# Forget gates' projection: high and low halves of eight weight columns in one stationary operand

## What is computed

```python
h = rmsnorm(x, norm_g[l])
proj = h @ w_in[l]
(cv_a, cv_b, cv_gate, fq, fk, fv, f_logit, fox_gate,
 mq, mem_gate) = jnp.split(proj, SPLITS, axis=-1)
...
logf = jax.nn.log_sigmoid(f_logit.astype(jnp.float32) + b_f[l].astype(jnp.float32))
y_fox = fox_attention(fq.reshape(shp), fk.reshape(shp), fv.reshape(shp), logf)
...
mkv = rmsnorm(mem, mem_norm_g[l]) @ w_mem_kv[l]
```

## Time and profile before

| | |
|---|---|
| median of 3 runs | 1925.85 us (1925.09 to 1926.88) |
| the profiled execution | 1928.19 us |
| its span, first to last instruction | 1926.4 us |
| busy: TensorE, VectorE, ScalarE, GpSimd | 98%, 58%, 40%, 10% |
| mean granted TensorE clock | 0.996 of full speed |
| the three products of a projection, 512 columns | 2288 of each, 931.8 + 893.9 + 894.4 us busy |
| chain that ended last | TensorE 81%, VectorE 7%, ScalarE 5% |
| transfers | 244.68 MB, mean 127 GB/s |

### The profile page before, as it was taken

How to read it: one execution, slowest core, us unless ns; L and a number is a source line. 1 busy time by engine, 2 the same in 40 slices (tenths; PEclk the granted TensorE clock), 3 DMA queues, 4 the chain that set the end, 5 groups by cost and what they waited for, 6 DMA issues and landing times.

```text
span 1926.4 us, 25228 instructions
## 1 busy us (share of the span) xinstructions
PE 1896.2 (98%) x8738; PEld 1546.8 (80%) x8738; DVE 1124.6 (58%) x1584; ACT 761.1 (40%) x1086; POOL 202.2 (10%) x201
## 2 busy tenths in 40 slices
PE   8999999999999999999999999999999999999999
PEld 6898888888888777887788888888888888887887
DVE  6664467777777767677633444344555555556332
ACT  6533333333333363323534334444454544553111
POOL 3500000000000002443100000000111111110000
PEclk9999999999999999999999999999999999999999
DMA  7244244444444426665122222222212222123441
GB/s 274 95 146 175 87 153 175 168 161 162 163 173 174 152 88 210 237 240 194 56 79 90 90 90 90 75 83 88 84 69 68 84 87 87 71 83 121 142 152 65
DMA packets 50406, 244.68 MB, mean 127 GB/s; under 512 B 5688, under 2 KB 6968, under 8 KB 29760
## 3 DMA queue, kind: packets, MB, share of 16 engines
q1 hardware_dynamic: 49920, 241.02, 35.2%
q10 hardware_dynamic: 448, 3.17, 0.4%
HBM read 235.75 MB, written 8.41 MB: 127 GB/s over the span
## 4 chain that ended last, share of the span: by engine, by line
PE 81%; DVE 7%; ACT 5%; issue 4%; POOL 2%; DMA 0%; SPq 0%; DVEq 0%; POOLq 0%; ACTq 0%
PE ps_p L551 24%; PE ps_p L553 23%; PE ps_p L552 23%; PE ps_s L633 2%; PE ps_o L651 2%; ACT w_hi L892 1%; PE ps_s L805 1%; DVE w_lo L1300 1%; PE ps_t L641 1%; POOL hz L2000 1%; POOL hz L2001 1%; ACT wk L907 1%; PE ps_x L570 1%; ACT wk L903 1%; DVE hb L1835 1%
## 5 line engine op out<-in xcount | busy, mean ns | idle before, releaser
L551 PE MATMUL ps_p<-act_hi,w_hi 128*128 128x512 f32 x2288 | 931.8, 407 | 5.8 <-DVE act_lo L1801 2.3
L553 PE MATMUL ps_p<-act_hi,w_lo 128*128 128x512 f32 x2288 | 894.4, 391 | 0.0
L552 PE MATMUL ps_p<-act_lo,w_hi 128*128 128x512 f32 x2288 | 893.9, 391 | 0.0
L551 PEld LDWEIGHTS ps_p<-act_hi,w_hi 128*128 128x128 f32 x2288 | 430.9, 188 | 96.2 <-issue 5.8
L553 PEld LDWEIGHTS ps_p<-act_hi,w_lo 128*128 128x128 f32 x2288 | 430.1, 188 | 92.0
L552 PEld LDWEIGHTS ps_p<-act_lo,w_hi 128*128 128x128 f32 x2288 | 431.2, 188 | 87.9 <-issue 5.3
L892 ACT ACTIVATE w_hi<-raw 128x2048 fp32r<-128x2048 f32 x154 | 294.4, 1912 | 425.8 <-PE ps_p L553 413.5
L1300 DVE TENSOR_TENSOR w_lo<-raw,w_hi 128x2048 fp32r<-128x2048 f32 x154 | 355.6, 2309 | 148.4 <-ACT w_hi L892 135.7
L1558 DVE CUSTOM_DVE_ANT_0 mkv<-mkv,c_all 128x1024 f32<-128x1024 f32 x96 | 146.0, 1557 | 0.5 <-DMA mkv<-ada_dram 0.2
L1982 POOL TENSOR_TENSOR ssq_a<-ssq_a,wk 128x512 f32<-128x512 f32 x15 | 38.4, 2561 | 745.5 <-ACT wk L1131 745.5
L2000 POOL TENSOR_TENSOR hz<-hqk,hd 128x128 f32<-128x128 f32 x56 | 38.6, 690 | 726.4 <-DVEq L1863 675.3
(11 more groups left out here) (282 smaller groups left out, 1763.0 us busy)
## 6 DMA issues: line engine op xcount, KB each, us to landing
raw<-wt_dram SPq DMA_DIRECT2D x156, 1024.0 KB, 4.8
mkv<-ada_dram SPq DMA_DIRECT2D x96, 512.0 KB, 4.7
qkv<-xT_dram SPq DMA_DIRECT2D x16, 256.0 KB, 2.8
spill_dram<-Y SPq DMA_DIRECT2D x16, 256.0 KB, 2.2
hqk<-spill_dram SPq DMA_DIRECT2D x16, 256.0 KB, 2.7
out_dram<-wk SPq DMA_DIRECT2D x16, 256.0 KB, 2.0
Y<-xT_dram SPq DMA_DIRECT2D x3, 1024.0 KB, 10.6
mem_raw<-memT_dram SPq DMA_DIRECT2D x4, 512.0 KB, 11.2
```

Source lines behind the costliest of these rows:

```text
L551: mm(o, wh, hi[:, k, 0:n], start=at == 0, stop=False)
L552: mm(o, wh, lo[:, k, 0:n], start=False, stop=False)
L553: last = mm(o, wl, hi[:, k, 0:n], start=False, stop=at == KT - 1)
```

## The change

The low halves of the eight forget-gate columns are written into the same stationary operand as the high halves, at columns 32 to 63 of each block; columns 8 to 31 are zero, so are their halves. Two products a contraction tile (against the high and the low part of the activations) then give the high rows at partitions 0 to 7 and the low rows at 32 to 39 of the PSUM bank. VectorE scales all 64 rows into SBUF, and one more fp32 product with a 0/1 matrix of 64 x 8 (`group_sum`, eight new columns of `cols`) adds the rows; it stands on TensorE's queue after contraction tile 4 of the first memory projection and waits for `flog_in`. VectorE does the split for the second memory tile in between, waits for `flog_full`, and adds the bias out of PSUM. In the second iteration of `conv` the split of the forget gates' tile is the narrow `split_beside`.

```diff
-                  ("one", 1), ("eps", 1), ("eps_square", 1)):
+                  ("one", 1), ("eps", 1), ("eps_square", 1), ("group_sum", NFOX)):
...
+            def flog():
+
+                s = slot("flog", 0)
+                pe.wait_ge(w_split, tile_no("flog", 0, 0) + 2)
+                pe.wait_ge(evac[s], half("flog", 0, 0) + 1)
+                for k in range(KT):
+                    w = w_hi[:, s, k * P:k * P + 64]
+                    mm(ps_p[0:64, s, :], w, act_hi[:, k, :], start=k == 0, stop=False)
+                    last = mm(ps_p[0:64, s, :], w, act_lo[:, k, :], start=False, stop=k == KT - 1)
+                    if k == 8:
+                        side("msum", 0, 0, mem_sum)
+                last.then_inc(proj_done, 1)
+
+            def flog_sum():
+
+                pe.wait_ge(flog_in, 1)
+                mm(ps_o[0:NFOX, :], cols[0:64, COLS["group_sum"][0]:COLS["group_sum"][0] + NFOX], wk[0:64, 0, :], start=True, stop=True).then_inc(flog_full, 1)
+
             def mem(i):
-                project("mem", i, 0, mem_hi, mem_lo, MEM)
+                project("mem", i, 0, mem_hi, mem_lo, MEM, hooks={4: flog_sum} if isinstance(i, int) else None)
...
-            project("flog", 0, 0, hooks={8: lambda: side("msum", 0, 0, mem_sum)})
+            flog()
...
+            def split_beside():
+
+                w = slot("flog", 0)
+                hi = w_hi[:, w, :].rearrange("p (k n) -> p k n", k=KT)
+                dve.wait_ge(w_hi_done, tile_no("flog", 0, 0) + 2)
+                tt(hi[:, :, 32:64], raw[:, w, :].rearrange("p (k n) -> p k n", k=KT)[:, :, 0:32],
+                   hi[:, :, 0:32].bitcast(F32), ALU.subtract).then_inc(w_split, 1)
+
...
-                split("conv", i, 1)
+                if i == 0:
+                    split("conv", i, 1)
+                else:
+                    split_beside()
...
-            do(tt(z8, ps_p[0:NFOX, s, :], r1[0:NFOX, :], ALU.mult))
+            do(tt(wk[0:64, 0, :], ps_p[0:64, s, :], r1[0:64, :], ALU.mult))
             dve.sem_inc(evac[s], 1)
-            do(ts(z8, z8, b_f, None, ALU.add))
+            dve.sem_inc(flog_in, 1)
+            split("mem", 0, 0)
+            dve.wait_ge(flog_full, 1)
+            do(ts(z8, ps_o[0:NFOX, :], b_f, None, ALU.add))
             dve.sem_inc(gate_in.sem, 1)
             do(ts(wk[0:NFOX, 2, :], z8, 0.0, None, ALU.min))
-            split("mem", 0, 0)
```

More of the change, by code:

```diff
@@ L305, in build @@
         ln_squares = sem("ln_squares")
+        flog_in = sem("flog_in")
+        flog_full = sem("flog_full")
         c_ready = sem("c_ready")
@@ L2070 @@
     put("eps_square", EPS * EPS)
+    put("group_sum", np.arange(P)[:, None] % 32 == np.arange(NFOX)[None, :])
     n = np.arange(P)
```

## The result

Over 22 runs of each, the changed kernel takes 1928.93 us (1926.71 to 1931.85) and the kernel before 1925.26 us (1924.59 to 1927.97): ratio 1.0017, 95% interval 1.0011 to 1.0024, that is +3.3 us (+2.1 to +4.6; the two medians themselves lie 3.7 us apart). The forecast was 1928.2 us, in a range of 1924.8 to 1930.2, as a time within 0.2% of before. The time lies in that range; the change makes the kernel slower, by less than 0.2% in the middle of the interval.

What follows compares the result with a forecast made beforehand. TensorE, busy 98% of the span, was taken as the bound. With the 0.1 us stall hidden, +0.6 us without the clock and +1.8 us for it made +2.4: 1925.85 + 2.4 = 1928.2 us, range 1924.8 to 1930.2.

Steps and rivals of the forecast that it cites:

- Removed, 3.63 us: Forget gates on TensorE: one of three products of each of 16 contraction tiles goes, 16 x 0.227 = 3.63 us.
- The wait, 3.1 us: First memory projection: TensorE idles from 109.8 to 112.9 us, 3.1 us, until VectorE's scaled copy is ready.
- (c): At the forget-gate hand-over: no wait worth the name, so the 2.7 us saving arrives, 1923.2 us; chance 0.04.
- The added product, 0.94 us: First memory projection, after contraction tile 4: one fp32 product of 512 columns costs 0.94 us, bounds 0.71 and 1.10.
- The chain behind it: ScalarE and VectorE behind the copy: work comes later, the third memory tile's split ending at 123.8 instead of 121.75 us.
- the stall of 0.1 us: Third memory tile: TensorE wants it at 123.7 us, its split ends at 123.8; 0.1 us, bounds 0 and 0.5.
- The sum without the clock: From the forget gates through the memory projections: +0.56 us at the hand-over and +0.1 us of stall, +0.7 us.
- The clock: After TensorE's idle gap: about 4 us at the lower clock level, costing +1.8 us, bounds 0 and 2.2.
- (b): At the hand-over: the same wait on VectorE, but the clock holds, 1926.6 us; chance 0.29.
- (d): First two memory projections: the clock falls and stays down while 256-column products run, +9 us, 1935; chance 0.06.
- (e): Forget gates: 64-column products already run at the lower level, 0.426 us each, +3.6 us, 1929.5 us; chance 0.04.

Runs made afterwards that it cites:

- Experiment 3: The changed kernel without the sum of the rows, low halves' contribution left out, VectorE's order as in the kernel before: 1925.78 us, ratio 1.0000.
- experiment 4: The changed kernel with tap 2 moved from ahead of the forget gates' copy to behind the minimum with zero: 1925.69 us, ratio 0.9998.
- experiment 5: The changed kernel with tap 2 moved, the sum after contraction tile 7, and ScalarE's and VectorE's work behind it reordered: 1923.72 us, ratio 0.9989.
- experiment 1: The changed kernel with 13 filler products on TensorE's queue right before its wait for VectorE's copy: 1926.75 us, ratio 1.0005.
- experiment 2: The changed kernel with the sum of the rows after contraction tile 15 of the first memory projection instead of tile 4: 1928.54 us, ratio 1.0014.
- run 8: The changed kernel, unchanged, profiled once more: 1928.85 us, the stretch 36.13 us.

## Why the prediction was right

**Removed, 3.63 us.** The memory projection starts 3.55 us earlier. The slot of a product with 64 stationary columns is a little longer than that with 128: from the gates' first product to the memory sum, (103.73 - 99.58) / 18 = 0.231 us instead of 0.227, which over 32 products is the missing 0.1. Right but for that.

**The wait, 3.1 us.** Measured 3.04 in three profiles, for the reason given: VectorE's taps are tied to the end of the convolution projections. Experiment 3 shows it without the added product, experiment 4 by moving a tap, experiment 5 by reordering what stands behind it as well. This was the step on which the forecast turned: whoever reads only that VectorE is busy for 58% of the span expects -2.7 us, and rival (c) was that.

**The added product, 0.94 us.** Counted as the prediction counted it, from its start to the second product behind it less one slot, it is (113.02 - 111.84) - 0.12 = 1.06 us at the full clock (experiment 1): a little more, inside the bounds of 0.71 and 1.10, and its 8 stationary columns make it no cheaper. At the lower clock the next product starts 1.81 us after it, as 0.94 + 0.9 had it.

**The chain behind it.** The third tile's split was put at 123.8 by the scale of the trace of before, 123.2 by that of the others, and ends at 123.15 where nothing else holds it (experiment 2). In the changed kernel itself it ends at 122.38 + 2.29 = 124.67, later than forecast, because ScalarE rounds that tile only when the first memory projection has ended, and the fallen clock makes that end the later of the two:

```profile
120.42 1.92 ACT L912 ACTIVATE w_hi<-raw 128x2048 fp32r<-128x2048 f32 x1 [1.47 <-PE ps_p L555]
```

TensorE wants the tile at 125.92, late by the same clock, so the stall of 0.1 us does not show, as foreseen. The sum without the clock, +0.7, is +0.71 in experiment 1, of which 0.67 are there at the first transpose (122.62 - 99.29 = 23.33 us after the mark instead of 22.66) and 0.04 are lost just behind it.

**The clock.** Priced at +1.8 us, with 4 us at the lower level. The three profiles have 3.4, 3.4 and 6.7 us, and the stretch less the 35.11 of the filled kernel gives +1.0, +1.2 and +2.6. The middle of these is under the price, the highest above the bound of 2.2: the bound was taken from 4.8 us of work at the lower level, and the trace of before held nothing longer; in the first profile the records are at the lower level from 112.33 to 118.57, 6.2 us of work. That term is the one that was mis-sized, in its spread rather than its middle. The page "TensorE: Matmul & The Clock Gate" of the Trainium skill (on HAM oscillation) says that the burst behind a long enough idle gap starts cold, and in its account of one kernel it lists the wait and the cost of the cold clock as two items. Experiment 1 agrees: it keeps the wait and takes away the second item, 1.0, 1.2 and 2.6 us against the three profiles.

**The rest.** The three stretches average +2.3 us, the runs +3.3 (2.1 to 4.6), and between the memory phase and 668 us the changed kernel is even 0.4 to 0.7 us shorter (last section), which nothing in the prediction had: so about 1.5 us are to be found elsewhere. The granted clocks of the runs point to where. Their mean is 0.9956 over the 22 runs of the changed kernel and 0.9974 over the 33 runs of the kernel before that were taken beside experiments 1 to 4, on another chip: 0.0018 x 2 x 1928 = 6.9 us more at the lower level in a run, of which the three profiles have 4.5 in the stretch. The other 2.4 us, which lie outside it, can cost up to 1.2 us; this is an estimate, since time at the lower level while TensorE waits costs nothing. One such place is behind the wait near 1757 us, where the clock had fallen in two of three profiles of the changed kernel and one of two before, 1.6 us each time. Why it would fall more often in the changed kernel stays open. That the forecast of +2.4 us lies near the measured +3.3 is thus in part luck: the mechanism and the sum without the clock are shown, but no profile had the 4 us at the lower level that the price assumed, and two effects outside the stretch, of opposite sign, were not foreseen.

**The rivals.** (b), a clock that holds, did not happen in the unfilled kernel in three profiles. (d) did not either, yet the first profile's 6.7 us were near its point of 7 us. (e) is ruled out by the starts: the last product of the gates at 107.15, the slot 0.231 us and not 0.426. (c) did not happen in the changed kernel; experiment 5 is what it takes to get there.

## What to carry to other kernels

Work taken from the bounding engine pays only until the next hand-over: before counting it, subtract how late the partner engine is there (here VectorE was 0.36 us late already, and its next split ended at 116.20, 1.05 us before the second memory tile wanted it at 117.25), and if the partner's start is tied to something that does not move, move the partner's work first. A new wait on that engine costs its idle time, and here waits of 2.0, 2.5 and 3.0 us (experiments 2 and 3, the changed kernel) were also followed by a spell at the lower clock that varies from run to run, while waits of 0.3 and 0.9 us (experiment 4) were not; filler products ahead of the wait take the second part away, and a better order takes both. To judge a change of some tenths of a per cent, measure the stretch it touches between two marks in the trace: in the kernel before it repeats to 0.01 us where whole runs spread over 3 us, and in the changed kernel it moves by 1.6 us with the clock, so take more than one profile.

## What was not expected of the hardware

The lower clock after one and the same idle time of 3.04 us lasted 3.4 us in two executions and 6.7 us in a third, and with it moved the cost of the wait from 1.0 to 2.6 us. After idle times of 2.04 to 2.1 us near 700 us the clock was 1.00 over 694 to 706 in the first profile of the kernel before and 0.86 in the second, with hardly a difference in time: from that product to the one behind the wait near 909 us it took 209.11 and 209.17 us. And between the memory phase and 668 us all kernels with two products for the forget gates run 0.4 to 0.7 us shorter than those with three (532.7 to 533.0 us against 533.39), although their code there is the same. The timelines of both kernels show no idle time of TensorE there. In run 8 the gain builds up by about 0.05 us in each of the eight iterations of the attention that uses the forget gates; the first profile of the changed kernel has 0.27 us more, from the fourth memory iteration. The cause is not known.
